# A ring of twelve weight slots for the experts, four of them in the memory of the transposed tokens

## The chip, the core and the metric

The kernel runs on one core of a Trainium2 chip. Its metric is the device time of one execution in microseconds, lower is better, given as the median of several runs. An engine name stands for its instruction queue: PE (TensorE) multiplies, ACT (ScalarE) and DVE (VectorE) work on elements, POOL (GpSimd) issues the indirect transfers here, SP (SyncE) issues nearly all weight transfers.

## What is computed

Two transformer blocks over 512 tokens of width 1024 in float32. The change touches only the last part of the second block, a mixture of experts in which each expert chooses its tokens:

```python
logits = jnp.einsum('bld,de->ble', u, w_router)
aff = jax.nn.softmax(logits, axis=-1)
top_aff, top_idx = lax.top_k(jnp.swapaxes(aff, 1, 2), cap)          # 16 experts, cap = 66 tokens each
xs = jax.vmap(lambda ub, ib: ub[ib])(u, top_idx)
hid = silu(einsum('becd,edf->becf', xs, w_gate)) * einsum('becd,edf->becf', xs, w_up)    # d 1024, f 512
y = einsum('becf,efd->becd', hid, w_down) * top_aff[..., None]
# y is added to the rows top_idx of the result, which is then normalised
```

Each expert has three weight matrices of 2 MB, so the 16 experts read 100.7 MB of weights (192 tiles of 512 KB).

## The kernel before

All weights of the kernel pass through one ring of `RING = 8` slots of SBUF (`ring_tile`, 128 partitions by 1024 float32 a slot, 512 KB). The class `Ring` writes the loads: SP waits until the semaphore `slot_free` has counted enough releases, issues one transfer of 512 KB into the next slot (L126), and the transfer's own semaphore (`slotK_loaded`) tells its readers. `slot_free` is one counter for the whole kernel: load number n waits for it to reach n + 1, and each reader that is done with a tile adds one, so at most eight tiles are loaded or on their way beyond those that PE has finished.

Before the experts, PE computes the output projection `w_out` in slices of tokens, transposes the new residual into `xT` (L2612) and multiplies it with the router's weights (L2628). The last of these multiplications raises `rt_l`. DVE then makes the softmax and finds the 66 best tokens of each expert (L2122 to L2177), while POOL copies the residual to `y_dram` (L3128) and writes the normalised rows to `u_dram` (L2197, L2199). When the first token numbers are there, POOL gathers the 66 rows of an expert from `u_dram` into `xs` (L2328, in the loop L2336), called a get below. `xT` isn't read any more after `rt_l`.

For each expert PE does a gate part and an up part, four tiles each (48 matmuls, L2224, L2229, L2230: the weights are split into an upper and a lower float32r part, so each product is three matmuls), and a down part (16 matmuls on four tiles, L2266). ACT makes the upper part of a gate or up tile (L2242, `ex_w_hi`), DVE the lower part in the slot itself (L2249), and only then may PE use it. Order on PE in the loop over pairs of experts: gate and up of expert e + 1, transposes of the tokens of expert e + 2 (L2209), down of expert e. SP loads in the same order: gate and up of expert 0 (`ex_first`), then gate and up of 1, down of 0, and so on. DVE scales the result (`ys`, L2309), and POOL adds its 66 rows to `y_dram` (L2317), called a put. POOL alternates: put of expert e, get of expert e + 4, put of expert e + 1; a get or a put is issued only when the one before it has landed. At the end `y_dram` is read back to `h`, normalised and written out (L443, L446).

Of the kernel before, what the change touches and what calls it, by code (L numbers as in the profile page):

```python
# [7 lines left out]
ACT, ALU, AX = mybir.ActivationFunctionType, mybir.AluOpType, mybir.AxisListType  # L8
# [15 lines left out]
SPLITS = 4  # L24
SPLITS2 = 2
EPS1, EPS2 = 1e-5, 1e-6
RING = 8
CAUSAL_COLS = [QT * P - P * i for i in range(QT)]
CAUSAL_AT = [sum(CAUSAL_COLS[:i]) for i in range(QT)]
CAUSAL = sum(CAUSAL_COLS)  # L30
# [20 lines left out]
UN = HEADS2 * T2  # L51
LAM_INIT = 0.8 - 0.6
O_AT = P
META_AT, XT_AT, XN_AT, OT_AT, STAGE_AT = 32896, 36992, 88256, 96448, 117536
EXPERTS, CAP, EXPERT_FF = 16, 2 * L2 // 16, 512
FT = EXPERT_FF // P
PICKS = 5
# [41 lines left out]
class Ring:  # L99


    def __init__(self, tile, loaded, free):
        self.tile, self.loaded, self.free = tile, loaded, free
        self.at, self.loads, self.plan, self.begin = 0, [0] * RING, {}, {}

    def load(self, sp, name, sources, turns=1):

        n, self.begin[name] = len(sources), self.at
        assert turns == 1 or n % RING == 0, (name, n)
        per = [0] * RING  # L110
        waits = []
        for j, s in enumerate(sources):
            slot = (self.at + j) % RING
            waits.append((slot, self.loads[slot], per[slot] + 1))
            per[slot] += s is not None
        self.plan[name] = [(slot, base, k, per[slot]) for slot, base, k in waits]

        def turn_loads(turn):
            for j, s in enumerate(sources):
                if s is None:  # L120
                    continue
                slot = (self.at + j) % RING
# [11 lines left out]
        for slot in range(RING):  # L134
            self.loads[slot] += per[slot] * turns

    def wait(self, pe, name, j, turn=0):
# [24 lines left out]
def build_program(nc, A, C, out):  # L162

    ctx = ExitStack()
    with ctx:
# [164 lines left out]
        with ExitStack() as branches:  # L330
# [21 lines left out]
        one_hot = at("one_hot", [P, 4, T2, CAP], XN_AT + 3200, BF16)  # L352
        aff_T, work, above, equal, count, ones_row = (at(name, [EXPERTS, L2], OT_AT + 4 * L2 * i) for i, name in enumerate(
            ("aff_T", "work", "above", "equal", "count", "ones_row")))
        ex_w_hi = at("ex_w_hi", [P, KT, D], STAGE_AT + 16896, F32R)
        u_rows = at("u_rows", [P, T2, D], STAGE_AT + 58880)
        w_out_hi = at("w_out_hi", [P, SPLITS2, D], STAGE_AT + 103264, F32R)
# [52 lines left out]
            sem(f"ex_{s}") for s in ("no", "xt", "xe", "gu", "sg", "h", "ht", "he", "y", "ye", "out"))  # L410

        ring = Ring(ring_tile, loaded, slot_free)
        NSA_CONST = 16 * 10
        B2_CONST, MOE_CONST = 16 * 12, 16 * 3

# [37 lines left out]
        def _(sp):  # L453
# [74 lines left out]
            def down(e):  # L528
                return [rows_tiles(wd, lambda t, k=k: e(t) * FT + k, lambda t: 0, D) for k in range(FT)]

            ring.load(sp, "ex_first", gate_up(lambda t: 0))
            ring.load(sp, "ex_loop", gate_up(lambda t: t * 2 + 1) + down(lambda t: t * 2)
                      + gate_up(lambda t: t * 2 + 2) + down(lambda t: t * 2 + 1), EXPERTS // 2 - 1)
            ring.load(sp, "ex_last", gate_up(lambda t: EXPERTS - 1) + down(lambda t: EXPERTS - 2) + down(lambda t: EXPERTS - 1))
            sp.wait_ge(u_row, T2)
            sp.dma_start(gain_bc[:, :], A["g_final_2"].partition_broadcast(P)).then_inc(gain_in, 16)
            finish(sp)
# [1540 lines left out]
                pe.matmul(bank[7][:, :], ident[:, :], h[:, 0, 0:512], start=True, stop=True)  # L2078

        def route_pe(pe):  # L2080
            pe.wait_ge(rt_a, 1)
            for t in range(T2):
                r = rows_of(t)
                dst = bank[1][0:EXPERTS, t * P:(t + 1) * P] if t < QT else bank[2][0:EXPERTS, 0:META]
                last = pe.transpose(dst, logits[0:r, t, :], ident[0:r, 0:r])
            last.then_inc(rt_at, 1)
            idle_turns_pe(pe, 17)
            pe.wait_ge(rt_s, 1)
            for t in range(T2):
                r = rows_of(t)  # L2090
                at = META + t * P if t < QT else 0
                last = pe.transpose(bank[3][0:r, t * EXPERTS:(t + 1) * EXPERTS], work[:, at:at + r], ident[0:EXPERTS, 0:EXPERTS])
            last.then_inc(rt_st, 1)
            pe.wait_ge(rt_p, 1)
            for e in range(EXPERTS):
                pe.wait_ge(rt_oh, e + 1)
                for t in range(T2):
                    r = rows_of(t)

                    last = pe.matmul(bank[4 if e < EARLY else 6][0:CAP, PICKS * e:PICKS * (e + 1)], one_hot[0:r, e % 4, t, :], token_aff[0:r, t, e, :],  # L2100
                                     start=(t == 0), stop=(t == QT))
                last.then_inc(rt_pk, 1)
            idle_turns_pe(pe, 2)
# [108 lines left out]
        def ex_gate_up_pe(pe, name, j, turn, i, u, m):  # L2212
# [4 lines left out]
            for k in range(KT):  # L2217
                n = m * (KT // 2) + k // 2
                if k % 2 == 0:
                    pe.wait_ge(ex_ws, e * KT + (n + 1))  # L2220
                    hi, lo = (w.rearrange("p (k n) -> p k n", n=512)
                              for w in (ex_w_hi[:, n, :], ring_lo[:, ring.plan[name][j + n][0], :]))
# [13 lines left out]
        def ex_split_act(act, name, j, turn, i, u, m):  # L2236
# [2 lines left out]
            if name != "ex_first":  # L2239
                act.wait_ge(ex_gate if m == 0 else ex_gu, e)  # L2240
            for n in range(m * (KT // 2), (m + 1) * (KT // 2)):
                act.activation(ex_w_hi[:, n, :], ring.wait(act, name, j + n, turn), ACT.Copy).then_inc(ex_wh, 1)  # L2242

        def ex_split_dve(dve, name, j, turn, i, u, m, tiles=None):

            for n in range(m * (KT // 2), (m + 1) * (KT // 2)) if tiles is None else tiles:
                slot = ring.plan[name][j + n][0]
                dve.wait_ge(ex_wh, i * (2 * KT) + (u * KT + n + 1))
                dve.tensor_tensor(ring_lo[:, slot, :], ring_tile[:, slot, :], ex_w_hi[:, n, :].bitcast(F32), ALU.subtract).then_inc(ex_ws, 1)  # L2249

        def ex_hidden_pe(pe, i, u):
            e = i * 2 + u
# [6 lines left out]
        def ex_down_pe(pe, name, j, turn, i, u, after_up=True):  # L2259
# [1 line left out]
            pe.wait_ge(ex_he, e + 2)  # L2261
            pe.wait_ge(ex_ye, e + 1)
            for k in range(FT):
                w = ring.wait(pe, name, j + k, turn)
# [634 lines left out]
        def _(act):  # L2899
# [55 lines left out]
                ex_split_act(act, "ex_last", 0, 0, EXPERTS // 2 - 1, 1, m)  # L2955
            ex_act(act, EXPERTS // 2 - 1, 1)
            for t in range(QT):
                act.wait_ge(tile_in[t], 32)
                act.activation(u_rows[:, t, :], h[:, t, :], ACT.Square, scale=D ** -0.5, accum_out=ssq[:, 0, t:t + 1]).then_inc(fin_sq, 1)


# [267 lines left out]
```

## Time and profile before

| | |
|---|---|
| median of 3 runs | 2655.4 us (2651.32 to 2655.63) |
| the profiled execution | 2657.1 us, of which its span is 2655.3 us |
| PE busy | 2446.6 us (92%) |
| DVE, ACT, POOL busy | 1327.8 us (50%), 902.8 us (34%), 1056.6 us (40%) |
| moved by DMA | 268.50 MB, 101 GB/s over the span |
| the experts, from the first gate matmul to the last put | about 2311 to 2639 us |

Times in the rows below are us from the span's start unless marked ns. The profile gives a granted clock of TensorE for each stretch, 1.00 being the upper level (2.4 GHz) and 0.50 the lower (1.2 GHz). A DMA share is the mean busy share of the core's 16 DMA engines; it can read a little over 1 where packets overlap.

### The profile page before, as it was taken

How to read it: one execution, taken by the hardware profiler on the slowest of the kernel's cores; microseconds unless marked ns; L12 is line 12 of the kernel's file. 1: busy time of each engine (PE TensorE's matmuls, PEld its weight loads, DVE VectorE, ACT ScalarE, POOL GpSimd, SP SyncE). 2: the span in 40 equal slices, each digit the busy share in tenths (PEclk: the TensorE clock that was granted, in tenths of full speed). 3: DMA queues.
4: the chain of work that ended last, by engine and by line, in shares of the span. 5: the costliest groups of instructions: out<-in, count | busy, mean ns of one | idle time of the engine just before them, and what ended most of it. 6: DMA issues, size and time to landing. Idle time of an engine off the chain costs nothing.

```text
span 2655.3 us, 36840 instructions
## 1 busy us (share of the span) xinstructions
PE 2446.6 (92%) x13805; PEld 1904.7 (72%) x13805; DVE 1327.8 (50%) x1992; ACT 902.8 (34%) x1691; POOL 1056.6 (40%) x1005
## 2 busy tenths in 40 slices
PE   6999899999998898899998799988989899799995
PEld 5777688888576656788887688868978897444442
DVE  3334255334464774434544465651167642667674
ACT  3344322222221674322224143331155301145452
POOL 7554444443024005444444544426831375411111
PEclk8999999999999999999999899989999999799998
DMA  4111333333241000333321211112201122389997
GB/s 130 56 55 49 96 95 95 95 95 95 67 116 64 1 1 25 103 96 100 97 88 45 62 41 41 56 33 72 87 25 33 40 87 66 131 301 354 349 354 249
DMA packets 267868, 268.50 MB, mean 101 GB/s; under 512 B 13339, under 2 KB 198518, under 8 KB 267750
## 3 DMA queue, kind: packets, MB, share of 16 engines
q1 hardware_dynamic: 262998, 253.91, 30.1%
q0 software_dynamic: 4752, 12.98, 2.0%
q8 instruction: 79, 1.29, 0.2%
q14 instruction: 39, 0.32, 0.0%
HBM read 256.10 MB, written 10.75 MB: 100 GB/s over the span
## 4 chain that ended last, share of the span: by engine, by line
PE 78%; DVE 9%; ACT 5%; DMA 4%; issue 3%; POOL 1%; SPq 1%; DVEq 0%; POOLq 0%; ACTq 0%
PE psum L2698 16%; PE psum L2702 16%; PE psum L2701 16%; PE psum L2266 3%; PE psum L1486 3%; PE psum L2343 2%; PE psum L2409 2%; PE psum L826 2%; DMA ring_tile<-in_w_up 2%; PE psum L2224 2%; PE psum L828 1%; PE psum L827 1%; PE psum L2229 1%; PE psum L2230 1%; PE psum L2352 1%
## 5 line engine op out<-in xcount | busy, mean ns | idle before, releaser
L2698 PE MATMUL psum<-x_hi,w_hi 128*128 128x264 f32 (+1 forms) x1536 | 526.1, 342 | 37.0 <-DVE x_lo L747 12.6
L2701 PE MATMUL psum<-x_lo,w_hi 128*128 128x264 f32 (+1 forms) x1536 | 515.8, 336 | 0.0
L2773 POOL TENSOR_TENSOR w_lo<-ring_tile,w_hi 128x1024 fp32r<-128x1024 f32 x128 | 307.9, 2406 | 381.2 <-ACT w_hi L2756 379.1
L785 POOL TENSOR_TENSOR w_hi<-ring_tile,one 128x256 fp32r<-128x256 f32 (+1 forms) x284 | 231.8, 842 | 502.3 <-PE psum L2702 463.4
L2698 PEld LDWEIGHTS psum<-x_hi,w_hi 128*128 128x128 f32 x1536 | 292.5, 190 | 74.9 <-issue 36.8
L2702 PE MATMUL psum<-x_hi,ring_tile_lo 128*128 128x264 f32 (+1 forms) x1088 | 340.2, 313 | 0.0
L2701 PEld LDWEIGHTS psum<-x_lo,w_hi 128*128 128x128 f32 x1536 | 292.9, 191 | 29.4 <-issue 1.2
L789 POOL TENSOR_TENSOR ring_tile_lo<-ring_tile,w_hi 128x256 fp32r<-128x256 f32 (+1 forms) x284 | 296.1, 1069 | 8.2
L2989 DVE TENSOR_TENSOR h<-psum,h 128x512 f32<-128x512 f32 x80 | 55.0, 691 | 337.3 <-PE psum L2702 270.1
L2756 ACT ACTIVATE w_hi<-ring_tile 128x1024 fp32r<-128x1024 f32 x128 | 134.9, 1056 | 251.7 <-PE psum L2702 240.9
L2702 PEld LDWEIGHTS psum<-x_hi,ring_tile_lo 128*128 128x128 f32 x1088 | 206.8, 190 | 11.8
L2702 PE MATMUL psum<-x_hi,w_lo 128*128 128x512 f32 x512 | 201.0, 393 | 0.0
L2701 PE MATMUL psum<-w_lo,hid_hi 128*128 128x512 f32 x512 | 199.2, 389 | 0.0
L2702 PE MATMUL psum<-w_hi,hid_lo 128*128 128x512 f32 x512 | 199.2, 389 | 0.0
L2698 PE MATMUL psum<-w_hi,hid_hi 128*128 128x512 f32 x512 | 199.2, 389 | 0.0
L2249 DVE TENSOR_TENSOR ring_tile_lo<-ring_tile,ex_w_hi 128x1024 fp32r<-128x1024 f32 x128 | 154.7, 1223 | 50.3 <-ACT ex_w_hi L2242 45.2
L3004 DVE TENSOR_TENSOR hid_lo<-hid_sq,hid_hi 128x512 fp32r<-128x512 f32 x64 | 168.8, 2637 | 2.2
L2242 ACT ACTIVATE ex_w_hi<-ring_tile 128x1024 fp32r<-128x1024 f32 x128 | 134.1, 1057 | 80.7 <-DMA ring_tile<-in_w_gate 42.6
L2883 ACT ACTIVATE relu<-psum 128x512 f32<-128x512 f32 x64 | 38.4, 599 | 262.1 <-PE psum L2702 262.1
L2224 PE MATMUL psum<-ring_tile_lo,xs_hi 128*66 128x512 f32 x256 | 109.4, 428 | 14.0 <-DVE ring_tile_lo L2249 14.0
L2266 PE MATMUL psum<-ring_tile,hid_T 128*66 128x512 f32 x256 | 112.7, 593 | 1.7 <-DVE hid_T L2301 1.7
L2702 PEld LDWEIGHTS psum<-x_hi,w_lo 128*128 128x128 f32 x512 | 97.3, 190 | 20.3
(425 smaller groups left out, 4993.0 us busy)
## 6 DMA issues: line engine op xcount, KB each, us to landing
ring_tile<-in_mlp_w SPq DMA_DIRECT2D x128, 512.0 KB, 3.9
ring_tile<-in_w_gate SPq DMA_DIRECT2D x64, 512.0 KB, 7.1
ring_tile<-in_w_up SPq DMA_DIRECT2D x64, 512.0 KB, 7.2
ring_tile<-in_w_down SPq DMA_DIRECT2D x64, 512.0 KB, 7.8
ring_tile<-in_w_in SPq DMA_DIRECT2D x52, 512.0 KB, 3.8
ring_tile<-in_sb_w_qkv SPq DMA_DIRECT2D x24, 512.0 KB, 3.8
ring_tile<-in_nsa_w_kv SPq DMA_DIRECT2D x12, 512.0 KB, 3.6
ring_tile<-in_sb_w_o SPq DMA_DIRECT2D x8, 512.0 KB, 3.5
```

What stands on the lines that cost most here:

```text
L785: last = pool.tensor_tensor(hi[:, cols], raw[:, cols], one[:, :].broadcast_to([P, D // len(parts)]), ALU.mult)
L789: last = pool.tensor_tensor(lo[:, cols], raw[:, cols], hi[:, cols].bitcast(F32), ALU.subtract)
L2224: first = pe.matmul(dst, xs_hi[:, u, k, :], lo[:, k % 2, :], start=(k == 0), stop=False)
L2242: act.activation(ex_w_hi[:, n, :], ring.wait(act, name, j + n, turn), ACT.Copy).then_inc(ex_wh, 1)
L2249: dve.tensor_tensor(ring_lo[:, slot, :], ring_tile[:, slot, :], ex_w_hi[:, n, :].bitcast(F32), ALU.subtract).then_inc(ex_ws, 1)
L2266: last = pe.matmul(bank[5 + n][0:CAP, :], hid_T[:, u, k, :], w[:, 512 * n:512 * n + 512], start=(k == 0), stop=(k == FT - 1))
L2698: upper = pe.matmul(dst, a_hi, b_hi, start=first, stop=False)
L2701: pe.matmul(dst, a_hi, b_lo, start=False, stop=False)
L2702: return pe.matmul(dst, a_lo, b_hi, start=False, stop=final)
L2756: act.activation(hi, raw, ACT.Copy).then_inc(split_w_hi, 1)
L2773: pool.tensor_tensor(lo, raw, hi.bitcast(F32), ALU.subtract).then_inc(split_w, 1)
L3004: dve.tensor_tensor(hid_lo[:, j, :], sq, hid_hi[:, j, :].bitcast(F32), ALU.subtract).then_inc(ff_hid, 1)
```

## The change

The experts' tiles get a ring of their own, `ex_ring`, with `EX_RING = 12` slots. Eight of them are the slots of the old ring at the same addresses, four more lie directly ahead of it in the last 16 KB a partition of `xT`. `follow` takes over the count of loads of the old ring, so that the first eight tiles of the experts go to the old eight slots in the same order as before and the next four to the new ones. Since `xT` is read until `rt_l`, PE waits for `rt_l` at the start of `route_pe` and then adds 4 to `slot_free`. The semaphores of the four new slots are `tile0_in` to `tile3_in`, which the start and the end of the kernel use too; the last use now waits for a higher count.

```diff
-RING = 8
+RING, EX_RING = 8, 12
...
-META_AT, XT_AT, XN_AT, OT_AT, STAGE_AT = 32896, 36992, 88256, 96448, 117536
+META_AT, XT_AT, EX_AT, XN_AT, OT_AT, STAGE_AT = 32896, 36992, 37504, 88256, 96448, 117536
...
+    def follow(self, ring):
+        more = self.size - ring.size
+
+        self.at, self.first, self.loads = ring.at, more + ring.at % ring.size - ring.at, [1] * more + ring.loads
...
-                slot = (self.at + j) % RING
+                slot = (self.first + self.at + j) % self.size
...
+        ex_tile = at("ex_tile", [P, EX_RING, D], EX_AT)
+        ex_tile_lo = at("ex_tile_lo", [P, EX_RING, D], EX_AT, F32R)
...
+        ex_ring = Ring(ex_tile, tile_in + loaded, slot_free)
...
-            ring.load(sp, "ex_first", gate_up(lambda t: 0))
-            ring.load(sp, "ex_loop", gate_up(lambda t: t * 2 + 1) + down(lambda t: t * 2)
+            ex_ring.follow(ring)
+            ex_ring.load(sp, "ex_first", gate_up(lambda t: 0))
+            ex_ring.load(sp, "ex_loop", gate_up(lambda t: t * 2 + 1) + down(lambda t: t * 2)
...
         def route_pe(pe):
+            pe.wait_ge(rt_l, 1)
+            pe.sem_inc(slot_free, EX_RING - RING)
             pe.wait_ge(rt_a, 1)
...
-                act.wait_ge(tile_in[t], 32)
+                act.wait_ge(tile_in[t], 16 * (ex_ring.loads[t] + 1))
```

The readers (`ex_gate_up_pe`, `ex_split_act`, `ex_split_dve`, `ex_down_pe`) only take `ex_ring`, `ex_tile` and `ex_tile_lo` in place of `ring`, `ring_tile` and `ring_lo`. No instruction changes its place on its engine; what changes is which semaphore some of them wait for. On PE, at the start of the routing, these are the rows of before (the last router products, then the transposes of the logits and the idle matmuls behind them):

```order
L2628 MATMUL psum<-router_w,xT 16x16 [waits norm_ev]
L2628 MATMUL psum<-router_w,xT 16x16 x3
L2085 MATMUL psum<-ident,logits 16x128 [waits rt_a]
L2085 MATMUL psum<-ident,logits 16x128 x3
L2085 MATMUL psum<-ident,logits 16x16
```

and these of the changed kernel, where the first transpose has `rt_l` ahead of `rt_a` in its waits (the addition to `slot_free` stands between the two and has no row):

```order
L2639 MATMUL psum<-router_w,xT 16x16 [waits norm_ev]
L2639 MATMUL psum<-router_w,xT 16x16 x3
L2096 MATMUL psum<-ident,logits 16x128 [waits rt_l,rt_a]
L2096 MATMUL psum<-ident,logits 16x128 x3
L2096 MATMUL psum<-ident,logits 16x16
```

On ACT, the upper parts of expert 1's gate tiles and the start of its up tiles, at the head of the loop, before:

```order
L2242 ACTIVATE ex_w_hi<-ring_tile 128x1024 [waits slot0_loaded]
L2242 ACTIVATE ex_w_hi<-ring_tile 128x1024 [waits slot1_loaded]
L2242 ACTIVATE ex_w_hi<-ring_tile 128x1024 [waits slot2_loaded]
L140 ISA
L2242 ACTIVATE ex_w_hi<-ring_tile 128x1024 [waits slot3_loaded]
L2242 ACTIVATE ex_w_hi<-ring_tile 128x1024 [waits slot4_loaded,ex_gu]
```

and in the changed kernel, where the four gate tiles lie in the new slots and the up tiles follow in the first old ones:

```order
L2253 ACTIVATE ex_w_hi<-ex_tile 128x1024 [waits tile0_in]
L2253 ACTIVATE ex_w_hi<-ex_tile 128x1024 [waits tile1_in]
L2253 ACTIVATE ex_w_hi<-ex_tile 128x1024 [waits tile2_in]
L2253 ACTIVATE ex_w_hi<-ex_tile 128x1024 [waits tile3_in]
L145 ISA [waits ex_gu]
L2253 ACTIVATE ex_w_hi<-ex_tile 128x1024 [waits slot0_loaded]
```

The work is the same; only the tile's slot and semaphore have moved.

## Rows read from the trace of the kernel before

**Rows 1.** The page: span, and DMA share in 40 slices.
```profile
span 2655.3 us, 36840 instructions
...
DMA  4111333333241000333321211112201122389997
```

**Rows 2.** Stretches: busy us by engine, granted clock, DMA share, GB/s.
```profile
core 0: us, PE busy (x) PEld busy (x) DVE busy (x) ACT busy (x) POOL busy (x), PEclk, DMA share, GB/s
...
2286.00:2298.00 12.00, 6.74 (x31) 3.50 (x29) 10.54 (x21) 0.00 (x0) 0.00 (x0) 0.86 0.00 1
...
2313.80:2344.50 30.70, 25.46 (x111) 15.13 (x110) 16.86 (x18) 10.23 (x12) 0.94 (x1) 0.87 0.73 237
2344.50:2370.00 25.50, 25.50 (x93) 11.69 (x92) 19.05 (x23) 13.72 (x17) 1.91 (x3) 1.00 0.94 323
2370.00:2596.70 226.70, 220.48 (x898) 110.97 (x896) 158.33 (x185) 111.15 (x126) 42.30 (x46) 1.00 1.04 352
```

**Rows 3.** Chain of work, 2344 to 2597: start, us, what.
```profile
2344.48 6.87 PE psum L2266 x16
...
2363.19 6.87 PE psum L2266 x16
2370.32 8.76 DMA ring_tile<-in_w_up
...
2383.58 6.87 PE psum L2266 x16
```

**Rows 4.** Timeline of PE, 2596 to 2634: down parts of experts 13 and 15.
```profile
2596.68 7.05 PE L2266 MATMUL psum<-ring_tile,hid_T 128*66 128x512 f32 x16
...
2623.84 7.08 PE L2266 MATMUL psum<-ring_tile,hid_T 128*66 128x512 f32 x16 [1.66 <-DVE hid_T L2301]
```

**Rows 5.** SP's own waits, 2200 to 2656: us in total, times, longest.
```profile
SPq L126 <- PE psum L2230: 146.0, 112, 50.0
```

**Rows 6.** Two of seven 4 us stretches with weight transfers only (396 to 410 GB/s).
```profile
2516.50:2520.50 4.00, 3.45 (x19) 1.94 (x19) 3.18 (x8) 1.15 (x3) 0.82 (x2) 1.00 1.03 396
...
2396.50:2400.50 4.00, 4.00 (x18) 2.20 (x17) 3.57 (x5) 2.08 (x2) 0.00 (x0) 1.00 1.03 410
```

**Rows 7.** Timeline of SP, 2204 to 2350: the experts' first transfers.
```profile
2232.94 30.60 SPq L126 DMA_DIRECT2D ring_tile<-in_w_up  x4
2313.86 5.20 SPq L126 DMA_DIRECT2D ring_tile<-in_w_gate  x4
```

**Rows 8.** Timeline, all engines, 2262 to 2312: routing.
```profile
2265.70 1.04 POOL L3128 DMA_DIRECT2D y_dram<-h  x1
...
2266.49 0.37 PE L2628 MATMUL psum<-router_w,xT 128*16 128x16 f32 x8 [0.32 <-DVE xT L2976]
...
2273.15 1.14 PE L2085 MATMUL psum<-ident,logits 128*16 128x128 f32 x5 [6.29 <-DVE logits L2134]
...
2298.07 5.94 POOL L2328 DMA_INDIRECT xs<-u_dram,pick_no  x1 [12.28 <-DVE pick_no L2166]
```

**Rows 9.** Timeline of POOL: put 2, get 6, put 3, and the last put.
```profile
2402.89 1.51 POOL L2317 DMA_INDIRECT y_dram<-ys,no_put  x1 [0.94 <-issue]
...
2411.77 0.97 POOL L2336 DMA_INDIRECT xs<-u_dram,no_get  x1 [7.17 <-DMA y_dram<-ys,no_put]
...
2420.98 1.50 POOL L2317 DMA_INDIRECT y_dram<-ys,no_put  x1 [8.04 <-issue]
...
2633.57 1.48 POOL L2317 DMA_INDIRECT y_dram<-ys,no_put  x1 [0.89 <-issue]
```

**Rows 10.** Landing of the get of 2324.9, and of the twelve in the loop.
```profile
L2328 POOL DMA_INDIRECT xs<-u_dram,pick_no x1: 937/937/937, 2324.9 to 2324.9; - x1
...
DMA to landing us min/median/max: 5.0/5.0/5.0
...
L2336 POOL DMA_INDIRECT xs<-u_dram,no_get x12: 969/970/1841, 2371.5 to 2584.6; - x12
...
DMA to landing us min/median/max: 6.8/8.3/8.9
```

More of the change, by code:

```diff
@@ L102, in __init__ @@
     def __init__(self, tile, loaded, free):
-        self.tile, self.loaded, self.free = tile, loaded, free
-        self.at, self.loads, self.plan, self.begin = 0, [0] * RING, {}, {}
+        self.tile, self.loaded, self.free, self.size = tile, loaded, free, len(loaded)
+        self.at, self.first, self.loads, self.plan, self.begin = 0, 0, [0] * self.size, {}, {}
+    def follow(self, ring):
+        more = self.size - ring.size
+        self.at, self.first, self.loads = ring.at, more + ring.at % ring.size - ring.at, [1] * more + ring.loads
     def load(self, sp, name, sources, turns=1):
         n, self.begin[name] = len(sources), self.at
-        assert turns == 1 or n % RING == 0, (name, n)
-        per = [0] * RING
+        assert turns == 1 or n % self.size == 0, (name, n)
+        per = [0] * self.size
         waits = []
         for j, s in enumerate(sources):
-            slot = (self.at + j) % RING
+            slot = (self.first + self.at + j) % self.size
             waits.append((slot, self.loads[slot], per[slot] + 1))
@@ L121, in turn_loads @@
                     continue
-                slot = (self.at + j) % RING
+                slot = (self.first + self.at + j) % self.size
                 sp.wait_ge(self.free, self.at + turn * n + j + 1)
@@ L133, in load @@
         self.at += n * turns
-        for slot in range(RING):
+        for slot in range(self.size):
             self.loads[slot] += per[slot] * turns
@@ L529, in down @@
                 return [rows_tiles(wd, lambda t, k=k: e(t) * FT + k, lambda t: 0, D) for k in range(FT)]
-            ring.load(sp, "ex_first", gate_up(lambda t: 0))
-            ring.load(sp, "ex_loop", gate_up(lambda t: t * 2 + 1) + down(lambda t: t * 2)
+            ex_ring.follow(ring)
+            ex_ring.load(sp, "ex_first", gate_up(lambda t: 0))
+            ex_ring.load(sp, "ex_loop", gate_up(lambda t: t * 2 + 1) + down(lambda t: t * 2)
                       + gate_up(lambda t: t * 2 + 2) + down(lambda t: t * 2 + 1), EXPERTS // 2 - 1)
-            ring.load(sp, "ex_last", gate_up(lambda t: EXPERTS - 1) + down(lambda t: EXPERTS - 2) + down(lambda t: EXPERTS - 1))
+            ex_ring.load(sp, "ex_last", gate_up(lambda t: EXPERTS - 1) + down(lambda t: EXPERTS - 2) + down(lambda t: EXPERTS - 1))
             sp.wait_ge(u_row, T2)
@@ L2221, in ex_gate_up_pe @@
                     hi, lo = (w.rearrange("p (k n) -> p k n", n=512)
-                              for w in (ex_w_hi[:, n, :], ring_lo[:, ring.plan[name][j + n][0], :]))
+                              for w in (ex_w_hi[:, n, :], ex_tile_lo[:, ex_ring.plan[name][j + n][0], :]))
                 dst = bank[2 + m][0:CAP, :]
@@ L2241, in ex_split_act @@
             for n in range(m * (KT // 2), (m + 1) * (KT // 2)):
-                act.activation(ex_w_hi[:, n, :], ring.wait(act, name, j + n, turn), ACT.Copy).then_inc(ex_wh, 1)
+                act.activation(ex_w_hi[:, n, :], ex_ring.wait(act, name, j + n, turn), ACT.Copy).then_inc(ex_wh, 1)
         def ex_split_dve(dve, name, j, turn, i, u, m, tiles=None):
             for n in range(m * (KT // 2), (m + 1) * (KT // 2)) if tiles is None else tiles:
-                slot = ring.plan[name][j + n][0]
+                slot = ex_ring.plan[name][j + n][0]
                 dve.wait_ge(ex_wh, i * (2 * KT) + (u * KT + n + 1))
-                dve.tensor_tensor(ring_lo[:, slot, :], ring_tile[:, slot, :], ex_w_hi[:, n, :].bitcast(F32), ALU.subtract).then_inc(ex_ws, 1)
+                dve.tensor_tensor(ex_tile_lo[:, slot, :], ex_tile[:, slot, :], ex_w_hi[:, n, :].bitcast(F32), ALU.subtract).then_inc(ex_ws, 1)
         def ex_hidden_pe(pe, i, u):
@@ L2263, in ex_down_pe @@
             for k in range(FT):
-                w = ring.wait(pe, name, j + k, turn)
+                w = ex_ring.wait(pe, name, j + k, turn)
                 for n in range(2):
```

## The prediction

> **What bounds the kernel now.** I read the page first. Its DMA line [rows 1] is low (0 to 4 tenths) for most of the span and stands at 8 to 9 only in the last sixth: only there can more slots for weights matter. So I cut that part into stretches [rows 2]. From 2370.0 to 2596.7 the DMA share is 1.04 at 352 GB/s, with PE at the upper clock (1.00) and busy for 220.48 of 226.70 us. Both are close to full, and one has to be the limit. Before it the DMA engines had room: share 0.94 from 2344.5 to 2370.0, 0.73 from 2313.8 to 2344.5, and nothing at all (1 GB/s) from 2286 to 2298.
>
> The chain of work tells who waits [rows 3]. The down parts of experts 0 and 1 start at 2344.48 and 2363.19, 18.71 us apart, with no wait for a weight between them: that is what an expert costs on PE. Then comes a piece of 8.76 us, the time from issue to landing of an up tile, and expert 2's down part starts 20.39 us after expert 1's. Expert 13's starts at 2596.68 [rows 4]. From expert 0 to 13 that is 252.20 us; 13 times 18.71 is 243.23. So PE loses **8.97 us** to late weights. From expert 2 to 13 the mean is (2596.68 - 2383.58) / 11 = 19.37 us. By bytes: an expert has 12 tiles of 0.524 MB, a get and a put of 66 rows of 4 KB, together 6.83 MB, which in 19.37 us is 353 GB/s, the rate of rows 2. The DMA engines are the bound there, short by 0.66 us per expert, and PE's loss is that shortfall added up. SP only waits for releases by PE [rows 5], so the ring is always full in the loop: more slots can't make transfers faster, they can only move some of them to an earlier time.
>
> **The change part by part.** *The four extra slots.* Before, SP issues the last of the first eight tiles by 2232.94 + 30.60 = 2263.5 and the next at 2313.86 [rows 7], when PE has released the first one. With the change, PE passes `rt_l` when the last router products end, 2266.49 + 0.37 = 2266.9 [rows 8], and expert 1's four gate tiles are issued at once, some 47 us earlier, ahead of a stretch with idle DMA engines. At 2313.8 twelve tiles are there instead of eight, all slots are full as before, and from then on each release by PE starts a transfer at the same moment as before, but of the tile four places on. So the unused share until 2370 (8.3 + 1.5 us of it) is not filled: releases set the pace there in both kernels. From 2370 on, where the DMA engines are the bound, they have four tiles less to do before any given tile.
>
> What four tiles are worth there has two ends. By themselves: stretches with only weights run at 396 to 410 GB/s [rows 6], 1.31 us for a tile at 400, 5.2 us for four. As a share of everything: 19.37 / 12 = 1.61 us a tile with the tokens' transfers in it, 6.5 us for four. The gets and puts are not fewer in the changed kernel, so the truth is near the first; but puts may slip ahead, since DVE reaches `ys` sooner when tiles aren't late, and a few moments in which the old ring let the DMA engines run dry close. I take **5.6 us**. It fits under the 8.97 us that PE can win back at all; 3.4 us of waits stay. At 0.66 us per expert the lead of 5.6 lasts some eight experts, so the waits should come back at about expert 10.
>
> The Trainium skill has its own figures for the rate: "DMA: Bandwidth & Descriptors", section Measured, gives 425 GB/s for one long stream of a single core, which would make the four tiles 4.9 us; "HBM Reference", section Specifications (TRN2), gives an effective 358 GB/s per core, which would make them 5.9 us. The 396 to 410 GB/s of the trace lie between.
>
> *The same tiles as a cost.* At 2267 they share the DMA engines with `y_dram<-h` (2 MB, issued at 2265.70) and the rows of `u_dram`, which the first get needs. All of that was over by 2286 [rows 2]; with 5.2 us more it is over by 2291.2, and the first get is issued at 2298.07, released by the token numbers from DVE [rows 8]. 6.9 us are left, so this costs nothing; if the cover were gone, each us beyond it would be a us on the end.
>
> *The wait for `rt_l` on PE and its addition.* PE sat idle for 6.29 us before its next matmul at 2273.15, waiting for DVE [rows 8]; two instructions of its queue lie in that. Zero. Nothing is queued behind them that could run sooner.
>
> *ACT, DVE, POOL, SP.* The same instructions in the same order. ACT's waits for expert 1's gate tiles are met long before, but it doesn't reach them sooner, since it takes them behind the tokens of expert 1: no gain there, the gain comes only from 2370 on. The last part (down of expert 15 at 2623.84, put at 2633.57 [rows 4, 9], read back, out) hangs on PE and moves as a whole.
>
> The sum: the profiled execution took 2657.1 us with a span of 2655.3, and would take 2657.1 - 5.6 = 2651.5. It lay 1.7 above the median of the runs; from the median, 2655.4 - 5.6 = **2649.8 us**.
>
> **The rivals.** *1, the lead is worth more: PE's floor.* A tile took 8.76 us from issue to landing [rows 3], at 1.61 us a tile some five were on the way; with four more the DMA engines may never run short, and the rate may rise by the 0.66 in 19.37 us (3.4%) that PE lacks. Then all 8.97 us go: 2646.4. For it: stretches of 410 GB/s exist. Against it: the share is 1.04 over 226.7 us, so there is little idle time to close. 0.15.
>
> *2, the opposite side: the tokens' chain takes over, slower.* POOL does put, get, put one after another, each only when the last has landed: 2402.89, 2411.77, 2420.98 [rows 9], 18.09 us per expert, just 0.62 under PE's 18.71. The get of 2324.9, with few tiles on the way, landed after 5.0 us, those in the loop after 8.3 [rows 10]. If a deeper queue of weights lengthens them again, POOL becomes the bound. A put can follow its down part's start by 9.7 us (2623.84 to 2633.57), the next get by 8.9 more, and lands 8.3 later, at 26.9; PE needs it at 36.9 (two experts less the transposes): 10.0 us of slack. If each transfer took 1.3 us more, the chain would have 20.7 us per expert and PE would lose 13 x (20.69 - 18.71) - 10.0 = 15.7 us instead of 8.97: 2662.2. It breaks even at 1.04 us more. Against it: within the loop the landing times only spread from 6.8 to 8.9, and a PE slowed to that degree would empty the weights' queue again. 0.07.
>
> The Trainium skill speaks on that in "DMA: Bandwidth & Descriptors", section Queues, rings and completion order: a DMA engine takes packets from its queues in turn. By that, the depth of SP's queue wouldn't matter to POOL's transfers.
>
> *3, no change: the rate falls a little.* The lead is 5.2 to 6.5 us over some 299 us of transfers; a rate lower by 1.8% (352 to about 346 GB/s), from more transfers in flight at once or from slots in another place, eats it whole: 2655.4. Nothing in the trace shows such a fall. This is also how the change could fail to do what it says: four tiles early, and the end where it was. 0.12.
>
> *4, the early tiles delay the first get.* Needs more than 6.9 us beside the `u_dram` rows, where 5.2 are added; at 10 us it would cost 3.1 and leave 2.5 of gain: 2652.9. 0.03.
>
> **How the numbers follow.** The forecast has 0.63, with its own range of 4.5 to 7 us off (2650.9 to 2648.4); rival 1 has 0.15, 2 has 0.07, 3 has 0.12, 4 has 0.03. The range of 8 in 10 takes in the forecast, rival 1 and the nearer part of rivals 3 and 4, and leaves out the far ends and rival 2: 2645.5 to 2655.0. About 0.2% (5.3 us) is what a measurement of this kernel can tell from no change; its three runs differ by 4.3 us. The forecast lies right at that mark: I put six tenths of its 0.63 beyond it, which with rival 1 gives 0.53 for faster. Slower is 0.07, from rival 2 and the tail of 3; the same has the 0.40 that are left.
>
> **What would show it.** Right: SP's row of `in_w_gate` transfers at about 2267 and up tiles at 2313.9; expert 0's down part still at 2344.5; 18.71 us from down part to down part until about expert 9 or 10; expert 13's at about 2591.1; DMA share and rate after 2370 as before; gets landing within 9 us. Wrong: a piece of `xs<-u_dram` in the chain of work ahead of the transposes (rival 2), experts all at 18.7 us to the end (rival 1), or waits for tiles from expert 4 or 5 on at a rate under 347 GB/s (rival 3).

## The result: slower by 0.56%

The changed kernel takes 2667.81 us at the median of five runs (2664.94 to 2673.98), the kernel before 2655.40 beside it (2651.32 to 2656.38). The medians differ by 12.4 us. The ratio, taken over all runs of both, is 1.0056 with a 95% interval of 1.0041 to 1.0070: 14.9 us more, between 10.9 and 18.6. The prediction was 2649.8 with a range up to 2655.0: the sign was wrong, and the time lies well outside.

The page of the profiled execution of the changed kernel (2664.94 us): span, busy time, DMA share.

```profile
span 2663.1 us, 36827 instructions
...
PE 2442.8 (92%) x13805; PEld 1901.0 (71%) x13805; DVE 1319.9 (50%) x1992; ACT 891.6 (33%) x1691; POOL 1106.3 (42%) x1005
...
DMA  4111333332241001333322111113201122599996
```

PE, DVE and ACT did no more than before. POOL is busy for 1106.3 us where it was 1056.6, a gain of 50 us without one new instruction. That is the first thing to follow up.

The early transfers came as described: in the timeline of SP, expert 1's gate tiles are issued at 2262, the up tiles when PE starts (in [rows 7] the four transfers after the first eight came at 2313.86).

```profile
2262.28 4.55 SPq L131 DMA_DIRECT2D ex_tile<-in_w_gate  x4
2308.80 5.00 SPq L131 DMA_DIRECT2D ex_tile<-in_w_up  x4
```

The chain of work of the changed kernel, 2330 to 2663, at the down parts of experts 0, 1, 6 and 7, against [rows 3]:

```profile
2339.24 6.87 PE psum L2277 x16
...
2357.99 6.87 PE psum L2277 x16
...
2461.45 9.51 PE psum L2277 x16
...
2482.83 6.87 PE psum L2277 x16
```

and the timeline of PE at expert 13, against [rows 4], with the transposes ahead of it:

```profile
2603.80 0.72 PE L2220 MATMUL psum<-ident,xs 66*128 66x66 f32 x8 [1.02 <-DMA xs<-u_dram,no_get]
2604.36 7.03 PE L2277 MATMUL psum<-ex_tile,hid_T 128*66 128x512 f32 x16
```

The experts' part began 5.2 us earlier than in the profiled execution of before (2339.24 against 2344.48; in the other kernels measured below that leave PE all of its work that moment lies anywhere between 2336 and 2350, so it says nothing on the change). From expert 0 to 13 it then took 2604.36 - 2339.24 = 265.1 us instead of 252.2, 12.9 more. 12.9 - 5.2 = 7.7, and the spans differ by 7.8: the whole loss is there. The first two steps from down part to down part are 18.7 us, as forecast; from expert 3's (2396.53, in PE's timeline) to 13's the mean is 20.78 us. The seventh down part (expert 6's) took 9.51 instead of 6.87 us: PE had waited for 2.9 us ahead of it, and the granted clock was 0.67 in the ten us from 2460.

What PE waited for stands in the view of waits, 2344 to 2610:

```profile
PE psum L2220 <- DMA xs<-u_dram,no_get: 15.1, 9, 2.9
```

Nine times it is the tokens, not a tile. Its counterpart by stretches shows 240.0 - 224.9 = 15.1 us without PE, and the DMA engines less in use than in the last line of [rows 2] (1.04, 352):

```profile
2364.00:2604.00 240.00, 224.90 (x893) 112.42 (x892) 150.87 (x186) 99.43 (x124) 85.62 (x46) 0.98 1.01 331
...
2460.00:2470.00 10.00, 9.69 (x23) 3.63 (x24) 8.06 (x10) 8.52 (x11) 4.10 (x3) 0.67 0.85 250
```

The waits are not the whole loss. From expert 1's down part to expert 13's it is 246.4 us (2358.0 to 2604.4), 21.8 more than 12 x 18.71. PE is idle in 15.1 of these; the other 6.7 are longer busy time for the same matmuls, at a granted clock that is 0.98 over the stretch and 0.67 where it is lowest (0.94 from 2420 to 2440 is the next). In the kernel before it was 1.00 [rows 2].

The chain of work shows who sets the pace, here from `ys` of expert 2 through its put and the get of expert 6 to the transposes of expert 6's tokens, which stand ahead of expert 4's down part:

```profile
2388.52 1.42 DVE ys L2320 x2
2390.26 6.29 issue
2397.02 1.51 POOLq L2346
2398.53 6.83 issue
2405.59 11.75 DMA xs<-u_dram,no_get
2417.47 0.72 PE psum L2220 x8
```

It runs through POOL, and a get lands 11.75 us after its issue; [rows 10] had 8.3 at the median. The line of the gets and its landings, of the changed kernel, against the same row in [rows 10]:

```profile
L2347 POOL DMA_INDIRECT xs<-u_dram,no_get x12: 972/5041/7137, 2363.2 to 2592.9; - x12
...
DMA to landing us min/median/max: 7.5/11.8/13.8
```

The growth isn't in the transfer. POOL's own instruction, which was 970 ns, now takes 5.04 us at the median, and the landing counts from its start. The timeline of POOL, in order of time (the last row is a get that was short):

```profile
2352.51 0.18 POOL L2326 COPY no_put<-pick_no 66x1 uint32<-66x1 uint32 x1 [31.82 <-DVE ys L2320]
2354.50 1.53 POOL L2328 DMA_INDIRECT y_dram<-ys,no_put  x1 [1.80 <-issue]
...
2382.13 7.14 POOL L2347 DMA_INDIRECT xs<-u_dram,no_get  x1 [7.03 <-DMA y_dram<-ys,no_put]
...
2396.82 1.51 POOL L2328 DMA_INDIRECT y_dram<-ys,no_put  x1 [6.55 <-issue]
...
2405.59 5.16 POOL L2347 DMA_INDIRECT xs<-u_dram,no_get  x1 [7.07 <-DMA y_dram<-ys,no_put]
...
2418.24 1.50 POOL L2328 DMA_INDIRECT y_dram<-ys,no_put  x1 [7.29 <-PE psum L2220]
...
2490.34 0.97 POOL L2347 DMA_INDIRECT xs<-u_dram,no_get  x1 [6.89 <-DMA y_dram<-ys,no_put]
```

and DVE at those moments (a split is DVE's instruction on one tile, the tile less its upper part; its two inputs both lie in SBUF):

```profile
2379.26 9.16 DVE L2260 TENSOR_TENSOR ex_tile_lo<-ex_tile,ex_w_hi 128x1024 fp32r<-128x1024 f32 x8
...
2405.28 4.62 DVE L2260 TENSOR_TENSOR ex_tile_lo<-ex_tile,ex_w_hi 128x1024 fp32r<-128x1024 f32 x4
...
2490.09 1.40 DVE L2320 TENSOR_SCALAR ys<-psum,aff_now 66x512 f32<-66x512 f32 x2
```

The get of 2382.13 was issued inside a burst of eight splits and took 7.14 us, until 2389.27; the burst ended at 2388.42. The get of 2405.59 came 0.3 us after four splits had begun and ended at 2410.75, 0.85 us behind them. The one of 2490.34, beside a DVE instruction with one input in PSUM, took 0.97 us. All other held gets of the loop end the same way, 0.84 to 0.87 us behind the last split of a burst. In the kernel before, DVE had to wait between two splits, because ACT had to wait for the tile. These are its waits from 2344 to 2600, and one get with the two splits around it:

```profile
DVE ring_tile_lo L2249 <- ACT ex_w_hi L2242: 43.2, 40, 3.4
...
2449.33 1.84 POOL L2336 DMA_INDIRECT xs<-u_dram,no_get  x1 [7.04 <-DMA y_dram<-ys,no_put]
...
2449.10 1.23 DVE L2249 TENSOR_TENSOR ring_tile_lo<-ring_tile,ex_w_hi 128x1024 fp32r<-128x1024 f32 x1 [1.59 <-ACT ex_w_hi L2242]
2450.72 1.23 DVE L2249 TENSOR_TENSOR ring_tile_lo<-ring_tile,ex_w_hi 128x1024 fp32r<-128x1024 f32 x1 [0.40 <-ACT ex_w_hi L2242]
```

The first split ended at 2450.33, and the pause of 0.40 us behind it was enough: the get ended at 2451.17, 0.84 us after that split, though the next was running by then. With twelve slots the tiles are there (ACT waits for them for 2.8 us in place of 76.1), and DVE runs four or eight splits without a pause.

So POOL's serial chain, put to get to put, is 8.77 + 12.65 = 21.42 us (2396.82, 2405.59, 2418.24) where [rows 9] gave 18.09, and PE needs one turn per 18.7.

### The profile page after: what moved, and what is told of

Same layout as the page of the kernel before. It is cut to its first block, busy times and chain, and to the rows that moved or that the text cites. A ratio compares the mean times of both kernels' runs of the same rounds, so it can differ in the third digit from the quotient of the medians.

```text
span 2663.1 us, 36827 instructions
## 1 busy us (share of the span) xinstructions
PE 2442.8 (92%) x13805; PEld 1901.0 (71%) x13805; DVE 1319.9 (50%) x1992; ACT 891.6 (33%) x1691; POOL 1106.3 (42%) x1005
## 4 chain that ended last, share of the span: by engine, by line
PE 74%; DVE 9%; ACT 6%; issue 5%; DMA 3%; POOL 1%; SPq 1%; POOLq 1%; DVEq 0%; ACTq 0%
PE psum L2709 16%; PE psum L2713 16%; PE psum L2712 16%; PE psum L1495 3%; PE psum L2354 2%; DMA xs<-u_dram,no_get 2%; PE psum L2420 2%; PE psum L835 2%; PE psum L837 1%; PE psum L836 1%; PE psum L2277 1%; ACT probs_a L1335 1%; ACT probs_b L1335 1%; PE psum L2363 1%; PE psum L1217 1%
## 5 line engine op out<-in xcount | busy, mean ns | idle before, releaser
L2260 DVE TENSOR_TENSOR ex_tile_lo<-ex_tile,ex_w_hi 128x1024 fp32r<-128x1024 f32 x128 | 147.1, 1215 | 0.0
L2253 ACT ACTIVATE ex_w_hi<-ex_tile 128x1024 fp32r<-128x1024 f32 x128 | 123.7, 1053 | 2.8 <-DMA ex_tile<-in_w_up 2.8
L2277 PE MATMUL psum<-ex_tile,hid_T 128*66 128x512 f32 x256 | 116.9, 611 | 1.7 <-DVE hid_T L2312 1.7
L2235 PE MATMUL psum<-ex_tile_lo,xs_hi 128*66 128x512 f32 x256 | 108.6, 424 | 7.8 <-DVE ex_tile_lo L2260 7.8
```

Of the source, the lines that this page charges most:

```text
L2253: act.activation(ex_w_hi[:, n, :], ex_ring.wait(act, name, j + n, turn), ACT.Copy).then_inc(ex_wh, 1)
L2260: dve.tensor_tensor(ex_tile_lo[:, slot, :], ex_tile[:, slot, :], ex_w_hi[:, n, :].bitcast(F32), ALU.subtract).then_inc(ex_ws, 1)
```

## The experiments

Each ratio is to the kernel before, timed on the same chip, with its 95% interval. Diffs are against the changed kernel; for runs with eight slots the whole change was taken back first. "0 to 13" is the time between the starts of the down parts of experts 0 and 13 (252.2 before, 265.1 after; 243.2 if PE never waits), read from the one execution that was profiled. e10 and e11 ran once each.

| run | median us | ratio | 0 to 13, us | loop's gets: POOL's instruction, ns min/median/max |
|---|---|---|---|---|
| e1_no_lead | 2656.40 | 1.0011 [1.0001, 1.0020] | 250.6 | 972/972/1497 |
| e2_short_split | 2641.65 | 0.9959 [0.9943, 0.9975] | 243.6 | 969/969/1252 |
| e3_half_loads | 2643.81 | 0.9963 [0.9949, 0.9976] | 243.2 | 972/2929/9192 |
| e4_plain_gets | 2644.16 | 0.9970 [0.9960, 0.9981] | 243.2 | 970/974/996 |
| e5_lead_two | 2650.82 | 0.9981 [0.9969, 0.9992] | 252.5 | 970/1761/5966 |
| e6_before_plain_gets | 2655.26 | 0.9999 [0.9988, 1.0010] | 252.1 | 969/972/1721 |
| e7_get_ahead | 2650.29 | 0.9984 [0.9974, 0.9994] | 249.4 | 976/2828/9456 |
| e8_psum_split | 2644.92 | 0.9968 [0.9955, 0.9982] | 243.2 | 969/970/997 |
| e9_plain_lead_two | 2646.84 | 0.9968 [0.9957, 0.9979] | 243.2 | 971/971/1706 |
| e10_less_pe_12, one execution | 2630.02 | | 237.7 | 967/971/2007 |
| e11_less_pe_8, one execution | 2648.87 | | 256.5 | 967/971/1839 |

**The second ring without its lead.**

```diff
         def route_pe(pe):
-            pe.wait_ge(rt_l, 1)
-            pe.sem_inc(slot_free, EX_RING - RING)
```

> The changed kernel without PE's wait for rt_l and its addition of 4 to slot_free: twelve slots at the new addresses and the new semaphores, but only eight tiles ahead, as before. Theory A (the lead lets DVE run its split instructions back to back, and a get's issue on POOL is held up by them): the time of before, 2655 +- 4, gets busy 1.0 us on POOL and landing in 8.3 us. Theory B (more transfers in flight lengthen the tokens' transfers): the same, since no more are in flight. Theory C (the place of the slots or their semaphores costs it): 2667 as with the change.

Twelve slots exist, but only eight are ever ahead. The time is 2.9 us above that of before (0.3 to 5.3), hardly more than nothing, the gets are short again and 0 to 13 is nearly that of before (250.6 against 252.2). Other slots and semaphores aren't the cause; of the 14.9 us, 12 come with the four tiles of lead.

**A short split on DVE.** The lower part is made for 128 of 1024 columns, and PE reads the upper part in its place.

```diff
-                              for w in (ex_w_hi[:, n, :], ex_tile_lo[:, ex_ring.plan[name][j + n][0], :]))
+                              for w in (ex_w_hi[:, n, :], ex_w_hi[:, n, :]))
...
-                dve.tensor_tensor(ex_tile_lo[:, slot, :], ex_tile[:, slot, :], ex_w_hi[:, n, :].bitcast(F32), ALU.subtract).then_inc(ex_ws, 1)
+                dve.tensor_tensor(ex_tile_lo[:, slot, 0:P], ex_tile[:, slot, 0:P], ex_w_hi[:, n, 0:P].bitcast(F32), ALU.subtract).then_inc(ex_ws, 1)
```

> The changed kernel with DVE's lower parts made over 128 of 1024 columns (0.2 us in place of 1.15) and PE reading the upper part in their place: it leaves out most of the lower parts of the experts' gate and up weights. The twelve slots and their lead stay. Theory A: the gets take 1.0 us on POOL again (median 5.0 with the change), land in about 8 us, the chain of puts and gets fits under PE's 18.7 us, and 9 us or more of the stage are won back: 2646 to 2650. Theory B: as many weights in flight as with the change, gets still land after about 11.8 us, 2660 or more.

The queue of weights stayed as deep, the gets became short (969 ns, landing after 8.2 us), and the time fell by 26 us against the changed kernel, to 11 below the kernel before. That removes the depth of the queue as the cause. It also made DVE faster altogether, so it doesn't yet single out the port of the second input.

**Half the bytes, eight slots.** The other way round: no lead and no full DMA engines, but tiles that are always early. Each transfer brings half a tile, ACT and PE read the loaded half twice, and DVE subtracts `ex_w_hi` from itself (the diff shows the down tiles and DVE only).

```diff
...
-                return [rows_tiles(wd, lambda t, k=k: e(t) * FT + k, lambda t: 0, D) for k in range(FT)]
+                return [half_tiles(wd, lambda t, k=k: e(t) * FT + k, lambda t: 0, D) for k in range(FT)]
...
-                dve.tensor_tensor(ring_lo[:, slot, :], ring_tile[:, slot, :], ex_w_hi[:, n, :].bitcast(F32), ALU.subtract).then_inc(ex_ws, 1)
+                dve.tensor_tensor(ring_lo[:, slot, :], ex_w_hi[:, n, :].bitcast(F32), ex_w_hi[:, n, :].bitcast(F32), ALU.subtract).then_inc(ex_ws, 1)
...
```

> The kernel before (eight slots), but each transfer of an expert's weight tile loads only half of its columns; ACT reads the loaded half twice, DVE makes an instruction of the same size from the upper parts, PE reads what is there. It leaves out half of the experts' weights and all of their lower parts. Tiles are always early and DVE's split instructions stand back to back, while few bytes are in flight. Theory A: gets take several us on POOL (median over 3), the down parts are over 18.71 us apart (20 or more at the median pair), and the time is not below 2655 though the DMA engines are half idle. Theory B: gets land in 5 to 7 us, all experts take 18.7 us, about 9 us less than before: 2646.

The long gets are there, longer than ever. Two stretches of this kernel's timeline, POOL's and DVE's:

```profile
2491.01 9.19 POOL L2346 DMA_INDIRECT xs<-u_dram,no_get  x1 [5.65 <-DMA y_dram<-ys,no_put]
...
2491.33 8.03 DVE L2259 TENSOR_TENSOR ring_tile_lo<-ex_w_hi 128x1024 fp32r<-128x1024 f32 x7
```

At a DMA share of 0.72 and 198 GB/s a get is held for 9 us by seven splits: what matters is that tiles are early, not how deep or how full the queue is. The seven splits ended at 2499.36; DVE paused for 0.25 us, and the get ended at 2500.20, 0.84 us behind them. The rest of the expectation failed: the median get, 2.9 us, stayed just under the 3 I had asked for, the down parts stayed 18.7 us apart, and the time was far below the 2655 that I had set as its least. Long gets mostly alternate with short ones here and puts land after some 6.4 us at the median, so the chain keeps up (puts two experts apart stand 36 to 40 us from each other where two experts are 37.4), and PE is busy for all of the 220 us from 2360. By this run a long get costs something only when the chain has no room for it.

**Gets and puts written out, without copies and drains.** POOL's loop copies the token numbers with a register as index and waits, by a drain, for all its transfers before the next (a put before a get and a get before a put). Written out, each takes its own column of `pick_no`, and a get goes out behind its put.

```diff
+        def ex_put_plain(pool, e):
+            if e:
+                pool.wait_ge(ex_out, e * 16)
+                pool.sem_inc(ex_done, 1)
+            pool.wait_ge(ex_ye, e + 2)
+            pool.indirect_dma_start(y_dram[:, :], bass.IndirectOffsetOnAxis(ap=pick_no[:, e:e + 1], axis=0), ys[:, e % 2, :], None,
+                                    compute_op=ALU.add).then_inc(ex_out, 16)
...
-            ex_put(pool, 0, 0)
-            with loop(pool, EXPERTS // 2 - 2) as turn:
-                ex_get(pool, turn + 2, 0)
-                ex_put_next(pool, turn, 1)
-                ex_get(pool, turn + 2, 1)
-                ex_put_next(pool, turn + 1, 0)
-            for e in range(EXPERTS - 3, EXPERTS):
-                ex_put_next(pool, e // 2, e % 2)
+            for e in range(EXPERTS):
+                ex_put_plain(pool, e)
+                if e + 4 < EXPERTS:
+                    ex_get_first(pool, e + 4)
```

> The changed kernel with POOL's loop of gets and puts written out, so that the token numbers are read in place: no copy of a number and no drain ahead of a get or put, so a get no longer waits for the put before it to land, nor a put for the get. Theory A: a get may still be held up on POOL by DVE, but it starts some 8 us earlier and has the time; PE waits for no tokens, the lead works as forecast: 2646 to 2650 (9 us under before at most). Theory B: the tokens' transfers are slow but overlap, so the same; this run tells whether the serial chain is what carries the loss. If it is not, 2660 or more.

All twelve slots with their lead, all of DVE's work, and 8.0 us less than before (5.0 to 10.6). Its stretch:

```profile
2366.00:2597.00 231.00, 231.00 (x944) 117.82 (x943) 162.99 (x201) 112.35 (x135) 56.66 (x24) 1.00 1.05 367
```

PE is busy in all of it, and the experts come 18.70 us apart to the end. Every other put, from expert 1's to expert 13's, is still held (5.58 us, until 1.36 behind four splits), which hurts nobody, since no get waits for their landing: the next get is issued 0.3 us after the put's instruction. So this run does not take the holds away; it takes away that the chain passes them on. It leaves out the copy and the drain together and does not tell them apart, but in the changed kernel's timeline the copy takes 0.7 us, while some 7 lie between it and the get, where only the drain stands. This is the version that beats both kernels.

**The same POOL code, eight slots.**

> The kernel before (eight slots) with POOL's gets and puts written out, without copies and drains. Theory A says that the eight-slot kernel waits for weights and not for tokens: 2653 +- 3, waits of PE for splits as before, DMA rate about 353 GB/s. Rival: the serial chain of tokens already cost before, by making puts late and their transfers collide with the weights: 2645 to 2649, which would make the four slots needless.

0.9999: on its own it brings nothing. Before the change, POOL's chain was no limit, and the weights' waits are all there (0 to 13 in 252.1).

**The second input from PSUM.** DVE does as many instructions of the same length, but subtracts what stands in a bank of PSUM.

```diff
-                dve.tensor_tensor(ex_tile_lo[:, slot, :], ex_tile[:, slot, :], ex_w_hi[:, n, :].bitcast(F32), ALU.subtract).then_inc(ex_ws, 1)
+                dve.tensor_tensor(ex_tile_lo[:, slot, :].rearrange("p (k n) -> p k n", k=2), ex_tile[:, slot, :].rearrange("p (k n) -> p k n", k=2), bank[7][:, :].unsqueeze(1).broadcast_to([P, 2, 512]), ALU.subtract).then_inc(ex_ws, 1)
```

> The changed kernel with DVE's second input of the split taken from PSUM in place of SBUF: it leaves out the right lower parts of the experts' weights, with instructions of the same size in the same number. If it is the second SBUF input of DVE that holds up POOL: gets take 1.0 us though DVE is as busy, time 2642 to 2648. If any busy DVE does it: gets take about 5 us, 2660 or more.

The same moment as in the changed kernel's timeline above, POOL and then DVE:

```profile
2381.55 0.97 POOL L2347 DMA_INDIRECT xs<-u_dram,no_get  x1 [6.97 <-DMA y_dram<-ys,no_put]
...
2378.77 9.13 DVE L2260 TENSOR_TENSOR ex_tile_lo<-ex_tile,psum 128x1024 fp32r<-128x1024 f32 x8
```

Eight splits without a pause, 9.13 us against 9.16, and the get that is issued into them takes 0.97 us instead of 7.14. DVE being busy is not the cause; its second input in SBUF is. It isn't the indirect transfer alone that is held, either: POOL's small copy of the token numbers took 4.40 us at 2366.84 in the changed kernel, inside four splits (2366.58 to 2371.20), and 0.18 at 2366.38 here, inside four as well. And the time is that of e4 (2644.9).

The Trainium skill, "SBUF — State Buffer", section Who interferes with whom, says that a DVE instruction with two inputs in SBUF takes its second one through a read interface that it shares with GpSimd, that this contends with GpSimd instructions that read SBUF, and that the order of issue decides who is blocked. The 4.40 and 0.18 us of the copy agree. It infers that the generation of a transfer's descriptors needs the write interface, and so would pass beside such an instruction: the indirect transfers here did not (7.14 against 0.97 us), and the measurement decides.

**A shorter lead.** `pe.sem_inc(slot_free, 2)` in place of the four, with POOL's loop as it is:

> The changed kernel with 2 in place of 4 added to slot_free: ten tiles ahead. Theory A (DVE's split instructions, back to back once tiles are early, hold up the gets' issue on POOL): a shorter lead is used up sooner, so some gets are held and some not; between the time of before and of the change, 2655 to 2667, with median POOL time of a get between 1.0 and 5.0 us. If two tiles of lead are harmless and four not, the loss has a threshold: under 2653 and gets at 1.0 us.

and with the gets and puts written out:

> Gets and puts written out, and ten tiles ahead in place of twelve. If a lead is used up by a fixed shortfall of 0.66 us per expert at 353 GB/s, two tiles (2.6 to 3.2 us) are used up by expert 6 or so and experts 0 to 13 take some 246 to 250 us: 2649 to 2651. If two more tiles on the way already let the DMA engines keep up with PE (365 GB/s), no waits come back: 243.2 us for experts 0 to 13, 2644 to 2646.

The first came out better than I had thought, 5.0 us under before (2.1 to 8.2): with less lead DVE keeps part of its pauses (ACT waits for tiles for 43.2 us in the loop; 2.8 with four tiles of lead, 73.4 with none), and fewer gets are held. The hold grows with the lead: 972 ns at the median without one, 1761 with two tiles, 5041 with four. The time doesn't go one way (2656.4, 2650.8, 2667.8), since the lead also takes away waits for weights. That the lead is used up by some expert isn't what the trace shows: the longest holds, 5.97 and 5.33 us, come late, at 2519 and 2539, and there PE waited 4.1 us for tokens. This execution (2653.2, 0 to 13 in 252.5) was slower than the median. With the chain out of the way two tiles do as much as four (0.9968 and 0.9970): both end at PE's floor.

**The get before the put.** POOL's order is turned round, get of e + 4 and then put of e, with drains as before.

```diff
+            ex_get_first(pool, 4)
...
-            with loop(pool, EXPERTS // 2 - 2) as turn:
-                ex_get(pool, turn + 2, 0)
-                ex_put_next(pool, turn, 1)
-                ex_get(pool, turn + 2, 1)
-                ex_put_next(pool, turn + 1, 0)
+            with loop(pool, EXPERTS // 2 - 3) as turn:
+                ex_get(pool, turn + 2, 1)
+                ex_put_next(pool, turn, 1)
+                ex_get(pool, turn + 3, 0)
+                ex_put_next(pool, turn + 1, 0)
...
```

> The changed kernel with POOL's order turned: the get of expert e + 4 stands ahead of the put of expert e, with the copies and drains left as they are. Each still waits for the one before to land. Theory A: the get now starts when expert e + 2's tokens are transposed, while DVE waits for the tokens' upper part, so it takes 1.0 us on POOL; put and get together fit in 18.7 us, 2643 to 2648. If the serial chain itself is too long (over 18.7 us per expert even with unheld gets), the gets still have some 25 us of slack, and only the last puts come late: 2650 or more.

I expected 2643 to 2648 and got 2650.3. The gets are needed later, but the chain is as serial as before, and they fall into bursts again (up to 9.5 us; one put took 9.8). It's the serial waiting that has to go, not the order.

**What the DMA engines can do.** One of the three products of each gate and up tile is left out on PE, so PE needs less and the transfers set the pace; the gets and puts are written out. Once with twelve slots, once with eight.

```diff
-                pe.matmul(dst, xs_lo[:, u, k, :], hi[:, k % 2, :], start=False, stop=False)
```

> Twelve slots, gets and puts written out, and on PE one of the three products of each gate and up block left out (the lower part of the tokens with the upper part of the weights), which takes PE to about 15.0 us per expert, so that transfers must be the bound. It measures what rate twelve slots reach. If 353 GB/s was the limit of the DMA engines: 350 to 355, 19.4 us per expert. If eight slots were what limited it: 370 to 400 GB/s, 17.1 to 18.5 us per expert.

> The same with eight slots. If the DMA engines' limit was 353 GB/s: 350 to 355 here too. If the number of tiles on the way sets the rate: less than with twelve slots on the same chip, by 5 GB/s or more; above 353 all the same, since PE gives slots back sooner.

Twelve slots first:

```profile
2375.00:2560.00 185.00, 165.17 (x596) 75.05 (x596) 133.03 (x158) 93.45 (x109) 42.91 (x20) 0.95 1.05 365
```

then eight:

```profile
2375.00:2560.00 185.00, 160.56 (x563) 71.48 (x561) 126.33 (x148) 88.64 (x102) 34.49 (x18) 0.94 1.03 346
```

PE is idle for 19.8 of 185 us in the first and for 24.4 in the second. With the transfers as the limit the rate is 365 GB/s with twelve slots and 346 with eight; 0 to 13 takes 237.7 and 256.5 us. Each ran once, but 19 us are far beyond what runs differ by. Neither expectation was met as it stood. Twelve slots stayed under the 370 to 400 GB/s that I expected if eight were the limit, so at 365 something else sets in. Eight slots stayed under 353, where I had expected more than that, since PE gives slots back sooner.

## Why the prediction was wrong

**The reading of the stage was half right.** The last sixth is where the slots matter, the weights come late there before the change, and PE loses 9 us: e3, e4, e8 and e9 take back all of it (0 to 13 in 243.2).

**"The DMA engines are the bound", 353 GB/s, was wrong.** That is the rate of a ring of eight slots. With ten or twelve slots the same engines carried 364 and 367 GB/s at shares of 1.05 and 1.05, and 6.83 MB in 18.70 us is 365: all that PE asks for. I took the share of 1.04 as full. It was 1.03 at 346 GB/s too, so it doesn't tell a limit from a queue that is too shallow. The step "they can only move some of them to an earlier time" fell with it: more transfers on the way did raise the rate.

**"I take 5.6 us" was too little, where the lead could work.** The term is worth 8.0 us (e4, 5.0 to 10.6), the 8.97 of rival 1 and not a lead that is used up by expert 10. Had the chain of the tokens stayed out of it, the forecast would have missed by some 3 us only.

**"ACT, DVE, POOL, SP. The same instructions in the same order", at no cost, is the step that failed.** The instructions were the same, their neighbours in time weren't. Early tiles join DVE's splits into bursts, the bursts hold POOL's gets, and POOL's chain had only 0.62 us per expert to spare. It took 20.78 us per expert instead, where PE needs 18.71. The sum should have had a term for POOL: 12 x (5.04 - 0.97) = 49 us of longer instructions, of which slack and spare time hide more than half. What is left, from expert 0 to 13, is 265.1 - 243.2 = 21.9 us with the lower clock in it; less the 8.97 of waits for weights that did go, that is the 12.9 us by which the stage grew.

**The sign was in the trace before.** The first get in [rows 8] took 5.94 us where the fourth, in [rows 10], took 0.94, and I used the row for its start alone. This is DVE at that moment, kernel before:

```profile
2297.66 5.44 DVE L2171 TENSOR_TENSOR one_hot<-slot_no,slot_T 128x330 bf16<-128x330 f32 x13
```

Thirteen instructions with two inputs in SBUF, until 2303.10; the get was released at 2304.01. The longest of the twelve gets in the loop (1841 ns in [rows 10]) is the one of 2449.33 above, held by a single split.

**The slack of 10.0 us was too large.** I took the put's distance of 9.7 us from expert 15, where nothing else is on DVE. In the loop `ys` stands behind up to eight splits: expert 0's put was issued at 2354.50, 15.3 us after its down part began. That leaves some 4.4 us of the 10.0, and expert 3 was already late. The rows of before had it too: put 2 at 2402.89 [rows 9] stands 19.3 us behind expert 2's down part at 2383.58 [rows 3].

**Rival 2 came true in its consequence and not in its cause.** It had the place (the chain put, get, put), the sign that I was to look for (a piece of `xs<-u_dram` ahead of the transposes) and nearly the price: 20.7 us per expert, measured 20.78. I gave it 0.07 because landings in the loop spread by 2 us only. But its mechanism, a deeper queue of weights, isn't what happened. Puts land after 7.8 us as before; for the get of 2405.59, 11.75 - 5.16 = 6.6 us of the landing lie behind POOL's instruction, and before it was 8.3 - 1.0 = 7.3. And e2 and e8 have the deep queue, and their gets land after 8.2 and 8.1 us.

**Right were** the early tiles at 2262 without harm to the first get, the free wait for `rt_l` on PE, and 18.7 us for the first steps. Rival 3 (a lower rate) would have to show late tiles; the 331 GB/s are low because PE waited for tokens and released tiles later.

What stays open is why the slots' rate depends on their number in just this way (346 to 353 GB/s for eight, 364 to 367 for ten and twelve); only the dependence was shown. With all of its work PE asks for no more than 365, but in e10, where it could take more, twelve slots gave 365 too. So that may be the limit of these transfers, just where PE's need lies; no run with more slots or a smaller mix of gets and puts shows it. Nor was it tried which of POOL's reads is the one that is held.

## What to carry to other kernels

When a wait goes away, ask what then runs without a pause, and whether another engine lived on those pauses: a serial chain with 3% to spare is a bound in waiting. Before calling a transfer-bound stretch full, compare its bytes per unit of work with its best stretches, since a busy share over 1 says nothing on whether more transfers in flight would help. And a single instruction that takes six times its usual time in the old trace is worth a look before it is used for its start alone.

## What the runs showed of the hardware that I had not expected

- An indirect transfer's instruction on POOL takes 0.97 us alone and up to 9.5 us if it falls among DVE instructions with two inputs in SBUF (9.8 for a put). It isn't let in between two that follow each other without a pause: a get ends 0.85 us behind the burst. A pause of 0.25 us (e3) or 0.40 us (before) let it in.
- A copy on POOL is held in the same way: 4.40 us against 0.18.
- A drain ahead of an indirect transfer waits until the transfers before it have landed: gets stood 7.0 us behind POOL's last instruction in its timeline, released by the put's landing; without drain and copy it was 0.3 us (e4).
- At nearly the same share (1.03 to 1.05) the DMA engines carried 346 and 352 GB/s with eight slots and 367 with twelve.
